# An output norm by two full-width ones-matmuls, one table set in the RWKV mixer, and work of ACT, DVE, POOL and PE moved at three stage borders

## The chip, the cores and the metric

The kernel runs on one core of one Trainium2 chip. The metric is the device time of one execution in microseconds (us). TensorE is written PE, VectorE DVE, ScalarE ACT, GpSimd POOL, SyncE SP.

## The reference

The input is 512 tokens by 1024 features, in float32. A first block (a gated convolution beside a state-space branch) is followed by two layers, each of them FFN, mixer, FFN; the mixer of layer 0 is a convolution beside RWKV-7, that of layer 1 is attention. Cut to what matters:

```python
def rms_norm(x, g):
    return x * lax.rsqrt(jnp.mean(x * x, axis=-1, keepdims=True) + 1e-6) * g

def hybrid_layer(x, pre_g, w_in, ..., w_out, post_g):      # the first block
    proj = rms_norm(x, pre_g) @ w_in
    ca, cb, z_c, u_s, z_s, g_c, g_s = split(proj)
    conv_out = (silu(layer_norm(conv(ca * sigmoid(cb)))) * silu(z_c)) @ w_conv_out
    y = gelu(s5_mimo(u_s, ...))
    y = y * sigmoid(y @ w_glu + b_glu)
    ssm_out = (y * silu(z_s)) @ w_ssm_out
    out = (sigmoid(g_c) * conv_out + sigmoid(g_s) * ssm_out) @ w_out
    return x + rms_norm(out, post_g)                       # the output norm

for layer in range(2):
    x = x + 0.5 * swiglu(rms_norm(x, g[0]), w_gate[layer, 0], w_up[layer, 0], w_down[layer, 0])
    x = x + mixer[layer](rms_norm(x, g[1]))                # RWKV and conv, then attention
    x = x + 0.5 * swiglu(rms_norm(x, g[2]), w_gate[layer, 1], w_up[layer, 1], w_down[layer, 1])

# in the RWKV mixer
kk = kk * lax.rsqrt(jnp.maximum(jnp.sum(kk * kk, axis=-1), 1e-24))
y = (y - mu) * lax.rsqrt(var + 64e-5) * ln_w + ln_b        # group norm over a head
```

## The kernel before

Activations lie transposed: eight tiles of 128 features by 512 tokens (`xT`). A product of float32 precision is made of two parts of each operand, a high one (the operand rounded to the PE's format) and a low one (what is left), in three rounds of matmuls: high weight by high activation, high weight by low activation, low weight by high activation. So each norm tile is made twice, `hH` by ACT (L388, L1420) and `hL` by DVE (L392, L1590). Each "unit" of weights, up to eight blocks of 128x128 that make one output tile, is loaded by SP into `w_raw`, split by ACT into `w_hi` (`split_hi`, L313) and by POOL into `w_lo` (`split_lo`, L321). The gate and up weights of an FFN are split by ACT (`gu_hi`, L607) and DVE (`gu_lo`, L616).

The work of every engine is one list of instructions, written out by hand, which runs in order; semaphores order the engines among each other. A `wait_ge` stops the engine, and all that stands behind it in its list. The changed lists stand at these places:

- **Start of block 1.** PE transposes `x_in`, ACT makes the eight `hH` (L1420), DVE the eight `hL`. PE then runs unit 0 (L1885, L1889, L1892: the three rounds), `raw_x(0)` (L1921, sixteen transposes that ACT copies to `xT`, L1432), unit 1, `params`, `raw_x(1)`, unit 2, the transposes of `srow` (L1941), unit 3, those of `Bblk` (L1949), unit 4. Between them ACT computes two sines (L1467, L1469), and DVE from these a chain of eleven small operations on `srow`, each of which waits for the one before it (L1642 to L1662); L1941 reads its last result. From unit 4 hang the state-space matrices and the convolution of the first block.
- **Output norm of block 1.** ACT squares each output tile (L1564), DVE adds the squares up (L1838). PE sums over the features by matmuls with a matrix of ones, one column per 128 tokens (L2051, L2054), ACT takes the root of a 128x4 tile (L1571), DVE its reciprocal (L1843) and four diagonal matrices (L1846), and PE spreads them over all rows (L2059) into `bank[7]`. DVE multiplies by it (`o_scale`, L1850), DVE (L1855) or POOL (L1382) adds the residual, and ACT and DVE make `hH` and `hL` of the first FFN.
- **First FFN (e = 0).** The first four gate/up units are "plain" (`plain_front` L1074 to L1086, `plain_back` L1098 to L1103), 512 tokens at once; later ones work on combined half-width tiles. For each unit DVE scales the gate by the norm's root R (`scale`, L877), ACT applies SiLU (L728), DVE multiplies by the up part (`gated`, L889), ACT makes the high part (`high`, L732), POOL the low part (L688). `norm_pe` (L423) sums the squares, ACT makes R by `Ln` and `Exp` (L738, L740). DVE also makes the sums that the combined units need (`state_sums`, L638 to L642; `turned_sum` L653; L588 to L592 on weights).
- **RWKV mixer.** For each of four head pairs, the preparation takes exponentials for the decays (L2267) and the root of the norm of `kk` (L2290, L2292). Then come triangular inverses over a chunk's tokens in levels, for two halves w = 0 and 1: PE L2757, L2777, with masks by POOL (L2238), while ACT, DVE make the group norm (L2323, L2328) of finished halves. POOL splits the units of the output product, `U_EO` and on, in between. The mixer ends with `group_affine` (L2338), `mix_hi` (L2313), the output product (L339 to L346), the residual (L2656) and the norm tiles of the next FFN; between these ACT and POOL split the last units, `U_EO + 4` and on. The gate/up units of the FFN behind (L1074 and on) follow.

## Time and profile before

| what | value |
|---|---|
| median of 3 runs | 2393.78 us (2391.64 to 2393.97) |
| the profiled execution | 2392.06 us |
| its span, from the first to the last instruction | 2390.2 us |
| mean granted TensorE clock | 0.998 |
| busy share of the span: PE, DVE, ACT, POOL | 98%, 71%, 47%, 37% |
| table loads of ACT | 48, each 1283 ns |

The span is the profiled execution less 1.9 us of start and end. A busy share counts the time in which an engine executes. In a row of the timeline the first number is when an instruction (or a run of equal ones, with "x" and their count) began, the second how long it lasted, and the brackets at the end say how long the engine had sat idle before it and what ended this.

### The profile page before, as it was taken

How to read it: one execution, taken by the hardware profiler on the slowest of the kernel's cores; microseconds unless marked ns; L12 is line 12 of the kernel's file. 1: busy time of each engine (PE TensorE's matmuls, PEld its weight loads, DVE VectorE, ACT ScalarE, POOL GpSimd, SP SyncE). 2: the span in 40 equal slices, each digit the busy share in tenths (PEclk: the TensorE clock that was granted, in tenths of full speed). 3: DMA queues.
4: the chain of work that ended last, by engine and by line, in shares of the span. 5: the costliest groups of instructions: out<-in, count | busy, mean ns of one | idle time of the engine just before them, and what ended most of it. 6: DMA issues, size and time to landing. Idle time of an engine off the chain costs nothing.

```text
span 2390.2 us, 42066 instructions
## 1 busy us (share of the span) xinstructions
PE 2335.4 (98%) x16891; PEld 1983.2 (83%) x16891; DVE 1698.9 (71%) x2282; ACT 1130.3 (47%) x1738; POOL 879.6 (37%) x533
## 2 busy tenths in 40 slices
PE   8999999999999999989999999999999999999999
PEld 6667767789899887877898998998998557898997
DVE  6999984297486479865884876865855776884771
ACT  5433353466265335334662654653644344562552
POOL 3799945322413446522114123132134212114123
PEclk9999999999999999999999999999999999999999
DMA  5222214223433332002334333342334221334333
GB/s 161 71 75 76 80 58 125 83 84 90 119 107 96 110 97 78 27 4 59 106 96 126 89 94 110 107 120 84 107 98 106 58 54 53 89 96 126 89 90 96
DMA packets 420789, 214.46 MB, mean 90 GB/s; under 512 B 17317, under 2 KB 419035, under 8 KB 420603
## 3 DMA queue, kind: packets, MB, share of 16 engines
q1 hardware_dynamic: 416523, 209.05, 30.9%
q10 hardware_dynamic: 4080, 2.83, 0.5%
q8 instruction: 129, 2.11, 0.4%
q14 instruction: 57, 0.47, 0.1%
HBM read 209.22 MB, written 2.10 MB: 88 GB/s over the span
## 4 chain that ended last, share of the span: by engine, by line
PE 76%; DVE 12%; POOL 7%; issue 2%; ACT 2%; DMA 0%; POOLq 0%; ACTq 0%; DVEq 0%
PE bank L1008 11%; PE bank L1014 10%; PE bank L1026 10%; PE bank L339 9%; PE bank L346 9%; PE bank L343 9%; POOL w_lo L321 3%; PE bank L1892 2%; PE bank L1889 2%; PE bank L1885 2%; DVE bank L1719 1%; PE bank L3436 1%; PE bank L2777 1%; POOL tmp L1352 1%; POOL tmp L1350 1%
## 5 line engine op out<-in xcount | busy, mean ns | idle before, releaser
L321 POOL TENSOR_TENSOR w_lo<-w_raw,w_hi 128x1024 fp32r<-128x1024 f32 (+5 forms) x276 | 534.5, 1942 | 568.4 <-ACT w_hi L313 566.1
L616 DVE TENSOR_TENSOR gu_w_lo<-gu_w,gu_w_hi 128x1024 fp32r<-128x1024 f32 (+1 forms) x254 | 364.1, 1436 | 92.4 <-ACT gu_w_hi L607 91.8
L688 POOL TENSOR_TENSOR ffn_aL<-tmp,ffn_aH 128x512 fp32r<-128x512 f32 x88 | 132.9, 1511 | 733.9 <-ACT ffn_aH L732 733.9
L313 ACT ACTIVATE w_hi<-w_raw 128x1024 fp32r<-128x1024 f32 (+5 forms) x276 | 235.8, 856 | 289.2 <-PE bank L346 272.5
L607 ACT ACTIVATE gu_w_hi<-gu_w 128x1024 fp32r<-128x1024 f32 (+1 forms) x254 | 299.5, 1183 | 30.2 <-DVE gu_w L590 19.4
L1008 PE MATMUL bank<-hH,gu_w_hi 128*128 128x256 f32 x1248 | 300.0, 279 | 0.0
L1014 PE MATMUL bank<-hL,gu_w_hi 128*128 128x256 f32 x1248 | 299.0, 279 | 0.0
L1008 PEld LDWEIGHTS bank<-hH,gu_w_hi 128*128 128x128 f32 x1248 | 231.5, 188 | 1.1 <-ACT tmp L724 0.5
L978 DVE TENSOR_TENSOR bank<-bank,R 128x512 f32<-128x512 f32 x64 | 44.7, 699 | 263.6 <-PE bank L346 263.6
L1014 PEld LDWEIGHTS bank<-hL,gu_w_hi 128*128 128x128 f32 x1248 | 231.0, 188 | 0.1
L1008 PE MATMUL bank<-st_hi,gu_w_hi 128*128 128x256 f32 x936 | 225.8, 280 | 1.1 <-ACT tmp L724 1.1
L1014 PE MATMUL bank<-st_lo,gu_w_hi 128*128 128x256 f32 x936 | 225.6, 280 | 0.0
L724 ACT ACTIVATE tmp<-bank 128x256 f32<-128x256 f32 x312 | 118.1, 378 | 181.0 <-PE bank L1026 180.9
L1026 PE MATMUL bank<-hH,gu_w_lo 128*128 128x256 f32 x1248 | 195.0, 278 | 0.0
L339 PE MATMUL bank<-ffn_aH,w_hi 128*128 128x512 f32 x704 | 181.1, 390 | 0.0
L346 PE MATMUL bank<-ffn_aH,w_lo 128*128 128x512 f32 x704 | 180.9, 390 | 0.0
L343 PE MATMUL bank<-ffn_aL,w_hi 128*128 128x512 f32 x704 | 180.4, 389 | 0.0
L1008 PEld LDWEIGHTS bank<-st_hi,gu_w_hi 128*128 128x128 f32 x936 | 173.5, 188 | 1.7 <-ACT tmp L724 1.7
L1014 PEld LDWEIGHTS bank<-st_lo,gu_w_hi 128*128 128x128 f32 x936 | 173.5, 188 | 0.0
L1026 PEld LDWEIGHTS bank<-hH,gu_w_lo 128*128 128x128 f32 x1248 | 167.1, 188 | 0.0
L1719 DVE SCALAR_TENSOR_TENSOR bank<-cu,par,bank 128x512 f32<-128x512 f32 x232 | 160.2, 741 | 0.0
L346 PEld LDWEIGHTS bank<-ffn_aH,w_lo 128*128 128x128 f32 x704 | 131.5, 188 | 28.6 <-POOL w_lo L321 1.6
(563 smaller groups left out, 4673.2 us busy)
## 6 DMA issues: line engine op xcount, KB each, us to landing
gu_w<-in_ffn_w_gate SPq DMA_DIRECT2D x88, 512.0 KB, 3.7
gu_w<-in_ffn_w_up SPq DMA_DIRECT2D x88, 512.0 KB, 4.8
w_raw<-in_w_in SPq DMA_DIRECT2D x48, 512.0 KB, 3.8
w_raw<-in_ffn_w_down SPq DMA_DIRECT2D x64, 384.0 KB, 3.6
w_raw<-in_ffn_w_down SPq DMA_DIRECT2D x64, 320.0 KB, 3.3
w_raw<-in_even_w_in SPq DMA_DIRECT2D x26, 512.0 KB, 3.9
w_raw<-in_w_conv_out SPq DMA_DIRECT2D x8, 512.0 KB, 4.0
w_raw<-in_w_out SPq DMA_DIRECT2D x8, 512.0 KB, 3.8
```

Of the source, the lines that this page charges most:

```text
L313: nc.scalar.activation(w_hi[u % 3][:, 0:K, :], w_raw[u % 4][:, 0:K, :], ACT.Identity).then_inc(w_hi_ready, 1)
L321: nc.gpsimd.tensor_tensor(w_lo[u % 3][:, 0:K, :], w_raw[u % 4][:, 0:K, :], w_hi[u % 3][:, 0:K, :].bitcast(F32), ALU.subtract).then_inc(w_l ...
L339: nc.tensor.matmul(out, H[:, k, :], sH[:, k0 + k, :], start=start and k == 0, stop=False)
L343: nc.tensor.matmul(out, H[:, k, :], sL[:, k0 + k, :], start=False, stop=False)
L346: ins = nc.tensor.matmul(out, L[:, k, :], sH[:, k0 + k, :], start=False, stop=stop and k == K - 1)
L607: nc.scalar.activation(gu_wh[v % 2][:, b0:b1, :, :], gu_w[v % 3][:, b0:b1, :, :], ACT.Identity).then_inc(gu_hi_ready, 1)
L616: nc.vector.tensor_tensor(gu_wl[v % 3][:, b0:b1, :, :], gu_w[v % 3][:, b0:b1, :, :], gu_wh[v % 2][:, b0:b1, :, :].bitcast(F32), ALU.subtra ...
L688: nc.gpsimd.tensor_tensor(aL[:, in_half(n), :], up_t[:, :], aH[:, in_half(n), :].bitcast(F32), ALU.subtract).then_inc(a_lo, 1)
L1008: nc.tensor.matmul(out, H[:, block, k, :], state_hi_lo(operand, k)[0], start=name in OPENS and k == 0, stop=False, skip_group_check=True)
L1014: nc.tensor.matmul(out, H[:, block, k, :], state_hi_lo(operand, k)[1], start=False, stop=False, skip_group_check=True)
L1026: ins = nc.tensor.matmul(out, L[:, block, k, :], state_hi_lo(operand, k)[0], start=False, stop=k == 3, skip_group_check=True)
L1719: ins = V.scalar_tensor_tensor(x_ if k == PAD else acc, x_, w_, acc, M, A)
```

## The change

1. **Start.** PE interleaves units 0 and 1 (`first_two`): for each of the eight `hH` a matmul of unit 0 and one of unit 1, the same over `hL`, then the low weights of unit 0, then those of unit 1. `raw_x(0)` comes behind both. ACT splits unit 1 ahead of the eight `hH`.
2. **Output norm.** Two ones-matmuls of 128x512 sum the squares over the features and leave the sum in every row; ACT makes the inverse root by `Ln` and `Exp` on 128x512. The column matmuls, the root of 128x4, the reciprocal, and the four diagonal matrices with their matmuls go. DVE's first `gu_lo` of unit 1 moves behind four low tiles, ACT's second `gu_hi` of unit 1 behind the first `hH`.
3. **First FFN.** `plain_front` waits for banks and weights one by one, where it uses them; `norm_pe` moves into the second unit's back part, between its gate and its up half; SiLU, `high` and copies on ACT, and `gated`, `scale`, `turned_sum` on DVE change places in the third to fifth unit.
4. **RWKV.** One table set, which holds the logarithm and the exponential, is loaded ahead of the decays; 12 of the 48 table loads go (8 at `kk`, 4 at the group norm).
5. **POOL's** splits of units `U_EO` and `U_EO + 1` move from before the masks of half 0 to between the halves.
6. **RWKV's tail.** ACT runs both `group_affine` of the last pair at once, and both `mix_hi` with one split between them; the splits of units `U_EO + 8` and `+ 9` come one norm tile earlier.

```diff
@@ ACT, first FFN
                 gu_hi(act, 1, 0)
-                gu_hi(act, 1, 1)
                 for j0 in (0, 4):
                     for j in range(j0, j0 + 4):
                         high_tile(act, gain(0, j), j, x_tile_new(j))
+                        if j == 0:
+                            gu_hi(act, 1, 1)
...
                         if e == 0 and v == 2:
+                            silu(n - 1)
                             state_high_act(act, e, 3)
+                            high(n - 1)
+                            continue
...
+                        if e == 0 and v == 3:
+                            turned_high_act(act, e)
+                            gu_hi(act, n + 1, 2)
+                            continue
...
+                    if e == 0 and c == 0 and v == 4:
+                        silu(n - 2)
+                        high(n - 2)
+                        gu_hi(act, n + 1, 0)
+                        copy(n, COPIES[1])
+                        silu(n - 1)
+                        copy(n, COPIES[2])
+                        high(n - 1)
+                        gu_hi(act, n + 1, 1)
+                        copy(n, COPIES[3])
+                        gu_hi(act, n + 1, 2)
+                        copy(n, COPIES[4])
+                        continue
@@ DVE, first FFN
                             state_sums_dve(v, e, 3)
+                            gated(n - 1)
                             gu_lo(v, n + 1, 0)
                             gu_lo(v, n + 1, 1)
-                            gated(n - 1)
...
+                        if e == 0 and v_ == 3:
+                            turned_sum_dve(v, e)
+                            scale(n - 1)
+                            gu_lo(v, n + 1, 1)
+                            turned_low_dve(v, e)
+                            gated(n - 1)
+                            continue
@@ PE, plain units
-            for n in ns:
-                ring_free(pe, n)
-                for which in range(2):
-                    free_banks(pe, n, which)
-                    pe.wait_ge(gu_hi_ready, part_no(n, which))
             for k in range(4):
                 pe.wait_ge(h_hi, q + k + 1)
                 for n in ns:
+                    if k == 0:
+                        ring_free(pe, n)
                     for which, block in ((0, 0), (1, 5)):
+                        if k == 0:
+                            free_banks(pe, n, which)
+                            pe.wait_ge(gu_hi_ready, part_no(n, which))
...
                             plain_back(pe, n)
-                            norm_pe(pe)
                         else:
-                            plain_back(pe, n)
+                            plain_back(pe, n, between=norm_pe)
@@ ACT, first block
             split_hi(act, 0)
+            split_hi(act, 1)
             act.wait_ge(setup_rd, PRE_RD)
             for j in range(DT):
                 act.wait_ge(setup_ps, XS_PS + j + 1)
                 s.activation(hH[:, j, :], bank[j][:, :], ACT.Identity, scale=pc("pre", j)).then_inc(h1_hi, 1)
-            split_hi(act, 1)
...
                 if j == 6:
-                    s.activation(rowst[:, 12:13], small[:, 0:1], ACT.Sqrt).then_inc(act_step, 1)
-                    act_sent(act_step)
+                    s.preload_act_table_set("natural_log_exp_and_others")
             act.wait_ge(ln_ps, O_PS)
-            s.activation(rowst[:, 0:4], bank[0][:, 0:4], ACT.Sqrt, scale=1.0 / D, bias=EPS6).then_inc(o_sq, 1)
+            s.activation(tmp[4][:, :], bank[7][:, :], ACT.Ln, scale=1.0 / D, bias=EPS6).then_inc(act_step, 1)
+            act.wait_ge(act_step, act_sent(act_step))
+            s.activation(bank[7][:, :], tmp[4][:, :], ACT.Exp, scale=-0.5).then_inc(o_sq, 1)
@@ DVE, output norm
-            v.wait_ge(o_sq, DT + 1)
-            V.reciprocal(rowst[:, 4:8], rowst[:, 0:4]).then_inc(dve_step, 1)
-            v.wait_ge(dve_step, dve_sent(dve_step))
-            for m_ in range(TT):
-                V.tensor_scalar(tmp[4][:, m_ * P:(m_ + 1) * P], ident[:, :], rowst[:, 4 + m_:5 + m_], None, M).then_inc(ln_gated, 1)
...
-            gu_lo(v, 1, 0)
-            v.wait_ge(ln_ps, R_PS)
+            v.wait_ge(o_sq, DT + 1)
...
                 if j0 == 0:
+                    gu_lo(v, 1, 0)
                     gu_lo(v, 1, 1)
@@ PE, first block
-            pe.wait_ge(h1_lo, 1)
-            w_in_unit(0, ready=(h1_lo, 0))
+            def first_two():
+                pe.wait_ge(h1_lo, 1)
+                pe.wait_ge(w_hi_ready, 1)
+                for k in range(DT):
+                    pe.wait_ge(h1_hi, k + 1)
+                    mm(w_in_bank(0)[:, :], w_hi[0][:, k, :], hH[:, k, :], start=k == 0, stop=False)
+                    if k == 0:
+                        pe.wait_ge(h1_lo, 2)
+                        pe.wait_ge(w_hi_ready, 2)
+                    mm(w_in_bank(1)[:, :], w_hi[1][:, k, :], hH[:, k, :], start=k == 0, stop=False)
+                for k in range(DT):
+                    pe.wait_ge(h1_lo, k + 1)
+                    for u in range(2):
+                        mm(w_in_bank(u)[:, :], w_hi[u][:, k, :], hL[:, k, :], start=False, stop=False)
+                for u in range(2):
+                    pe.wait_ge(w_lo_ready, u + 1)
+                    for k in range(DT):
+                        ins = mm(w_in_bank(u)[:, :], w_lo[u][:, k, :], hH[:, k, :], start=False, stop=k == DT - 1)
+                    ins.then_inc(unit_done, 1)
+
+            first_two()
             raw_x(0)
-            w_in_unit(1)
...
-            pe.wait_ge(o_sq, 5)
             pe.wait_ge(o_sum, DT - 2)
-            for m_ in range(TT):
-                mm(bank[0][:, m_:m_ + 1], tmp[3][:, m_ * P:(m_ + 1) * P], ones[:, 0:1], start=True, stop=False)
-                if m_ == 0:
-                    pe.wait_ge(o_sq, DT)
-                ins = mm(bank[0][:, m_:m_ + 1], tmp[7 % 3][:, m_ * P:(m_ + 1) * P], ones[:, 0:1], start=False, stop=True)
-            ins.then_inc(ln_ps, 1)
-            pe.wait_ge(o_sq, DT + 1)
-            for m_ in range(TT):
-                pe.wait_ge(ln_gated, DIAG + m_ + 1)
-                mm(bank[7][:, m_ * P:(m_ + 1) * P], ones[:, :], tmp[4][:, m_ * P:(m_ + 1) * P], start=True, stop=True).then_inc(ln_ps, 1)
+            mm(bank[7][:, :], ones[:, :], tmp[3][:, :], start=True, stop=False)
+            pe.wait_ge(o_sq, DT)
+            mm(bank[7][:, :], ones[:, :], tmp[7 % 3][:, :], start=False, stop=True).then_inc(ln_ps, 1)
@@ POOL, RWKV
-            for u in range(U_EO, U_EO + 2):
-                split_lo(pool, u)
             for w in range(2):
+                if w:
+                    for u in range(U_EO, U_EO + 2):
+                        split_lo(pool, u)
@@ ACT, RWKV
+                s.preload_act_table_set("natural_log_exp_and_others")
                 act.wait_ge(rw["csum"], J + 1)
...
             group_affine(1, 0)
+            group_affine(1, 1)
             split_hi(act, U_EO + 4)
-            group_affine(1, 1)
             act.wait_ge(rw["done"], 3)
             mix_hi(6, rT[:, 2, :])
-            split_hi(act, U_EO + 5)
             act.wait_ge(rw["done"], 4)
             mix_hi(7, rT[:, 3, :])
+            split_hi(act, U_EO + 5)
...
-                if U_EO + n_ + 2 < U_F[1]:
+                if n_ not in (6, 7) and U_EO + n_ + 2 < U_F[1]:
                     split_hi(act, U_EO + n_ + 2)
+                if n_ in (5, 6):
+                    split_hi(act, U_EO + n_ + 3)
```

The lists of PE at the start, where a row is an instruction with its line, its output and inputs and its count, read before:

```order
L1885 MATMUL bank<-hH,w_hi_55 128x512 x8
L1889 MATMUL bank<-hL,w_hi_55 128x512 x8
L1892 MATMUL bank<-hH,w_lo_57 128x512 x8
L1921 MATMUL bank<-ident,x_in 128x128 x16
L1885 MATMUL bank<-hH,w_hi_56 128x512 x8
L1889 MATMUL bank<-hL,w_hi_56 128x512 x8
L1892 MATMUL bank<-hH,w_lo_58 128x512 x8
L1927 MATMUL bank<-ident,prow 128x128 x2
```

and in the changed kernel, whose lines have other numbers (L1912 is L1885 of before, L1948 is L1921, L1954 is L1927; "..." leaves out the pairs that follow in the same way, over `hH` and then over `hL`):

```order
L1962 MATMUL bank<-hH,w_hi_55 128x512
L1966 MATMUL bank<-hH,w_hi_56 128x512
...
L1974 MATMUL bank<-hH,w_lo_57 128x512 x8
L1974 MATMUL bank<-hH,w_lo_58 128x512 x8
L1948 MATMUL bank<-ident,x_in 128x128 x16
L1954 MATMUL bank<-ident,prow 128x128 x2
L1948 MATMUL bank<-ident,x_in 128x128 x16
L1912 MATMUL bank<-hH,w_hi_59 128x512 x8
```

The first `raw_x` (sixteen `x_in` transposes) moved from behind unit 0 to behind unit 1; `params` (`prow`) stands directly ahead of the second `raw_x`, as before.

DVE's list at the output norm before, from the reciprocal on:

```order
L1843 RECIPROCAL rowst<-rowst 128x4
L1846 TENSOR_SCALAR tmp_70<-ident,rowst 128x128 x4
L616 TENSOR_TENSOR gu_w_lo_82<-gu_w_79,gu_w_hi_85 128x1024
L1850 TENSOR_TENSOR oT<-oT,bank 128x512
L1855 TENSOR_TENSOR xT<-xT,oT 128x512
L1850 TENSOR_TENSOR oT<-oT,bank 128x512 x2
L1855 TENSOR_TENSOR xT<-xT,oT 128x512
L1850 TENSOR_TENSOR oT<-oT,bank 128x512
L392 SCALAR_TENSOR_TENSOR hL<-xT,par,hH 128x512 x4
L616 TENSOR_TENSOR gu_w_lo_82<-gu_w_79,gu_w_hi_85 128x1024
```

and in the changed kernel, from the first multiplication of the output by the root on:

```order
L1877 TENSOR_TENSOR oT<-oT,bank 128x512
L1882 TENSOR_TENSOR xT<-xT,oT 128x512
L1877 TENSOR_TENSOR oT<-oT,bank 128x512 x2
L1882 TENSOR_TENSOR xT<-xT,oT 128x512
L1877 TENSOR_TENSOR oT<-oT,bank 128x512
L392 SCALAR_TENSOR_TENSOR hL<-xT,par,hH 128x512 x4
L616 TENSOR_TENSOR gu_w_lo_82<-gu_w_79,gu_w_hi_85 128x1024 x2
```

The reciprocal and four diagonal tiles are gone, and the split of `gu_w_lo_82` moved from ahead of the first multiplication to behind the four low tiles `hL`.

ACT's list at the end of the RWKV mixer before, from the first of the last two mixed tiles on (`w_hi` 128x256 and 128x1024 are splits of units, `hH` and the squares in `tmp` the norm tiles):

```order
L2313 ACTIVATE mixH<-rT 128x512
L313 ACTIVATE w_hi_56<-w_raw_54 128x256
L2313 ACTIVATE mixH<-rT 128x512
L313 ACTIVATE w_hi_59<-w_raw_51 128x256
L388 ACTIVATE hH<-xT,par 128x512
L378 ACTIVATE tmp_69<-xT 128x512
L313 ACTIVATE w_hi_55<-w_raw_52 128x256
L388 ACTIVATE hH<-xT,par 128x512
L378 ACTIVATE tmp_67<-xT 128x512
L313 ACTIVATE w_hi_56<-w_raw_53 128x1024
L388 ACTIVATE hH<-xT,par 128x512
L378 ACTIVATE tmp_68<-xT 128x512
```

and in the changed kernel, from the same tile on:

```order
L2352 ACTIVATE mixH<-rT 128x512 x2
L313 ACTIVATE w_hi_56<-w_raw_54 128x256
L313 ACTIVATE w_hi_59<-w_raw_51 128x256
L388 ACTIVATE hH<-xT,par 128x512
L378 ACTIVATE tmp_69<-xT 128x512
L313 ACTIVATE w_hi_55<-w_raw_52 128x256
L313 ACTIVATE w_hi_56<-w_raw_53 128x1024
L388 ACTIVATE hH<-xT,par 128x512
L378 ACTIVATE tmp_67<-xT 128x512
L313 ACTIVATE w_hi_59<-w_raw_54 128x1024
L388 ACTIVATE hH<-xT,par 128x512
```

The two mixed tiles now follow each other, and the splits of 128x1024 into `w_hi_56` and `w_hi_59` moved ahead of the norm tiles 1 and 2 that they stood behind.

## Rows read from the trace of the kernel before

**Rows 1.** The page, busy time of each engine over the span.

```profile
PE 2335.4 (98%) x16891; PEld 1983.2 (83%) x16891; DVE 1698.9 (71%) x2282; ACT 1130.3 (47%) x1738; POOL 879.6 (37%) x533
```

**Rows 2.** Busy time in two stretches: PE, PEld, DVE, ACT, POOL, granted clock, DMA, GB/s.

```profile
85.00:307.00 222.00, 216.78 (x918) 155.64 (x916) 221.92 (x325) 80.44 (x113) 214.57 (x143) 1.00 0.26 74
...
476.00:478.00 2.00, 2.00 (x6) 1.56 (x5) 2.00 (x3) 0.52 (x1) 1.45 (x1) 0.51 0.04 8
```

**Rows 3.** The timeline of PE at the start.

```profile
15.89 3.67 PE L1885 MATMUL bank<-hH,w_hi 128*128 128x512 f32 x8 [0.95 <-DVE hL L1590]
...
19.40 2.00 PE L1889 MATMUL bank<-hL,w_hi 128*128 128x512 f32 x8
...
23.07 1.91 PE L1921 MATMUL bank<-ident,x_in 128*128 128x128 f32 x16
...
37.81 0.42 PE L1941 MATMUL bank<-ident,srow 16*128 16x16 f32 x4
...
45.56 0.71 PE L1885 MATMUL bank<-hH,w_hi 128*128 128x512 f32 x2
```

**Rows 4.** The timeline of ACT, DVE and POOL at the start.

```profile
27.78 0.29 ACT L1469 ACTIVATE srow<-srow 16x128 f32<-16x128 f32 x1
...
31.77 0.27 DVE L1642 TENSOR_TENSOR srow<-srow 16x128 f32<-16x128 f32 x1
...
34.52 2.38 DVE L1660 TENSOR_TENSOR srow<-srow 16x128 f32<-16x128 f32 x1
...
36.93 0.28 DVE L1662 TENSOR_TENSOR srow<-srow 16x128 f32<-16x128 f32 x1
...
34.22 2.53 POOL L321 TENSOR_TENSOR w_lo<-w_raw,w_hi 128x1024 fp32r<-128x1024 f32 x1 [2.74 <-ACT w_hi L313]
```

**Rows 5.** The timeline at the output norm, and L738, L740 of the next norm.

```profile
466.20 0.38 PE L2054 MATMUL bank<-ones,tmp 128*128 128x1 f32 x2 [0.57 <-ACT tmp L1564]
...
469.05 2.05 PE L2059 MATMUL bank<-tmp,ones 128*128 128x128 f32 x8 [1.05 <-DVE tmp L1846]
...
469.40 1.22 DVE L616 TENSOR_TENSOR gu_w_lo<-gu_w,gu_w_hi 128x1024 fp32r<-128x1024 f32 x1
...
471.13 0.69 DVE L1850 TENSOR_TENSOR oT<-oT,bank 128x512 f32<-128x512 f32 x1 [0.51 <-PE bank L2059]
...
496.56 0.67 ACT L738 ACTIVATE tmp<-bank,small 128x512 f32<-128x512 f32 x1
...
497.26 0.63 ACT L740 ACTIVATE R<-tmp 128x512 f32<-128x512 f32 x1
```

**Rows 6.** The timeline of PE and DVE in the first FFN.

```profile
493.30 1.13 PE L423 MATMUL bank<-tmp,ones 128*128 128x512 f32 x2 [0.74 <-DVE tmp L383]
...
512.14 2.08 PE L1074 MATMUL bank<-hH,gu_w_hi 128*128 128x512 f32 x8 [1.01 <-issue]
...
532.24 0.73 PE L1008 MATMUL bank<-hH,gu_w_hi 128*128 128x256 f32 x4
...
511.85 2.25 DVE L588 TENSOR_TENSOR gu_w<-gu_w 128x1024 f32<-128x1024 f32 x1
```

**Rows 7.** The timeline in the RWKV mixer, DVE and PE.

```profile
968.98 2.88 DVE L2495 TENSOR_TENSOR prep<-prep,prep 128x512 f32<-128x512 f32 x1
...
977.96 1.16 PE L2757 MATMUL bank<-a_w,b_w 64*64 64x64 f32 x64 [0.34 <-DVE vT L2437]
```

**Rows 8.** The timeline at the RWKV mixer's end, ACT, DVE and PE.

```profile
1105.05 1.28 ACT L2328 ACT_TABLE_LOAD   x1
...
1106.34 1.15 ACT L2328 ACTIVATE tmp<-tmp 128x512 f32<-128x512 f32 x2
...
1123.69 1.45 DVE L392 SCALAR_TENSOR_TENSOR hL<-xT,par,hH 128x512 fp32r<-128x512 f32 x1 [0.86 <-ACT hH L388]
...
1122.16 2.11 PE L339 MATMUL bank<-mixH,w_hi 128*128 128x512 f32 x8 [1.11 <-ACT w_hi L313]
...
1155.89 2.19 PE L1074 MATMUL bank<-hH,gu_w_hi 128*128 128x512 f32 x8
```

13 lines of the change are left out of this document (9 added, 4 removed).

## Prediction

> **What bounds the kernel now.** I read the page's busy shares first: PE is busy for 2335.4 us of a span of 2390.2, 98% [rows 1]. All that a reordering can give is the remaining 55 us, and only where a wait of PE is removed and not made again behind it. Then I read the busy time by stretches, to see where another engine sets the pace. From 85 to 307 us DVE is busy for 221.92 of 222.00 us and POOL for 214.57 [rows 2]: there DVE decides, and PE (216.78) follows. So the start, which comes before that stretch, is worth exactly what it moves DVE's full stretch, whose input comes from unit 4 of PE at 45.56 [rows 3]. The list of PE's waits then gave the other places: the output norm, three plain units, the RWKV mixer and its end [rows 5 to 8]. No edit touches the long stretches in which PE is full.
>
> One thing in the trace bears on nearly all edits. DVE's chain at the start has steps of 0.27 to 0.28 us at 31.77 and 36.93, but the step at 34.52 lasted 2.38 [rows 4]. POOL had begun a `w_lo` at 34.22 that lasted 2.53, to 36.75, and the DVE step ended at 36.90, with it. The same shows in other stages: a 128x1024 operation of DVE that takes 1.22 at 469.40 [rows 5] took 2.25 at 511.85 [rows 6], and a 128x512 one of the preparation took 2.88 at 968.98 [rows 7]. So a DVE step on tiles in SBUF waits for a POOL operation that is under way; what is moved in time may be gained on PE and lost there.
>
> **The change part by part.** The sum is made against the profiled execution, 2392.06 us, which is 1.72 under the median of 2393.78; what the sum gives I add to the median.
>
> *Start.* The first eight matmuls over `hH` took from 15.89 to 19.40, 3.51, and the two dense rounds behind them from 19.40 to 23.07, 1.83 each [rows 3]: 1.68 of waiting for ACT. In the changed list sixteen matmuls share the eight `hH`. They need 3.66 dense; ACT makes the last `hH` at about 19.4, and two matmuls follow it, so they end near 19.9, and 0.35 of waiting stays. PE gains 1.68 - 0.35 = **1.3** by the end of unit 1. Against this, `raw_x(0)`, which began at 23.07 [rows 3], comes one unit later, about 27.2: ACT, which copies it and then makes two sines, of which the second ended at 28.07 [rows 4], has them at 23.07 to 27.2 = 4.1 less what its queue had in reserve, some 3.3 later: 31.35. That alone costs nothing, since DVE began on them only at 31.77 [rows 4]. But ACT's next weight split stands behind the sines, and with it POOL's `w_lo`: one now lies at about 32.5 to 34.9 and one at 35.45 to 37.85, and the chain of eleven DVE steps, which met one, meets both. Eleven steps of 0.31 (a step with its gap: 31.77 to 34.52 are nine) with two blocked ones end near 38.9; they ended at 37.21. L1941, which began at 37.81, begins at about 39.1 where PE is ready at 36.45. PE had no slack there, so the 1.3 is lost, and unit 4 begins at 46.2 to 46.4 where it began at 45.56 [rows 3]: **+0.8**. Ends: -1.3 if the second POOL operation misses the chain; if the next chain on DVE is hit as well, two blocked steps of 2.1 each (2.38 - 0.28) less the gain, +2.9. I take the replay.
>
> *Output norm.* Before: the column matmuls began their last part at 466.20, the spreading matmuls at 469.05, and DVE's first multiplication started at 471.13 [rows 5]. After: the last of two ones-matmuls begins at 466.20; a pair of these took 1.13 [rows 6], so I take 1.0; `Ln` and `Exp` cost 0.67 and 0.63 on the same shape [rows 5]; with the hand-overs `o_scale` starts at 468.65, 2.5 earlier. Behind it stands DVE: its `gu_lo` of 1.22 lay in the hole at 469.40 [rows 5] and now stands behind four low tiles with nothing to hide it. What reaches the second half of the norm is 2.5 - 1.2 = **1.3**. The granted clock adds a limit: it was 0.51 in 476 to 478 [rows 2], the lower level of 1.2 GHz after PE had stood still before these matmuls, and PE stands still at the new norm too; what PE does earlier there it does at that level.
>
> *First FFN.* If PE follows DVE's lead, its waits of 0.74 at 493.30 and 1.01 at 512.14 [rows 6] go as well: -1.3 - 0.74 - 1.01 = -3.1, the lower end. But DVE is the one that is full here, and its lead is 1.3. POOL's `st_lo` get ahead of DVE's steps as at 511.85, where one such meeting cost 2.25 - 1.22 = 1.0 [rows 6]; two more would leave -1.3 + 2.0 = +0.7, the upper end. I follow the chain to the matmul at 532.24 [rows 6], where the combined units' copies on ACT stand behind SiLU, `high` and weight splits, and take **-1.2** for norm and FFN together, near DVE's own lead. From 545 on PE is full and carries this to the mixer. The cover for the added Ln and Exp on ACT is nil, they are in the chain and in the sum; ACT's moved `gu_hi` lies in its waits for `hH`.
>
> *RWKV.* Eight loads fewer in the preparation (1.28 each [rows 8]) are hidden: ACT waits for DVE in each pair. In the last pair they let DVE end earlier; it ran late, blocked by four `w_lo`, as the row of 2.88 shows, and PE waited 0.34 for it at 977.96 [rows 7] and shortly at three places behind. Both loads of the last pair are worth at most 2 x 1.28 = 2.6, and nothing if POOL's lock hides them again. Loads of the group norm between two levels free some tenths more. The two moved `w_lo` of POOL now lie beside DVE's level steps of half 0's end, where one blocked step costs up to 2.1, of which I let 0.4 through, since DVE waits for PE there anyway. Together **-1.0** (ends: -2.6 and +0.5).
>
> *The mixer's end.* ACT's load at 1105.05 (1.28) lay between the root of the group norm and all that follows, and PE waited 1.11 at 1122.16 for the split of `U_EO + 8` [rows 8]. Both go: -2.4, the lower end. But POOL's `w_lo` follow ACT's splits. They come one tile earlier, among the low tiles and sums of DVE's norm: the low tile at 1123.69 lasted 1.45 beside such a `w_lo` [rows 8], twice the 0.69 that a step of as many elements takes at 471.13 [rows 5]. In my replay the two moved `w_lo` block one step each of 1.2 to 1.5, and the first unit of the next FFN, PE at 1155.89 [rows 8], which hangs on this DVE chain through ACT's weight split, comes 1.3 *later*. Between -2.4 and +1.3 I take **0**.
>
> Sum: +0.8 - 1.2 - 1.0 + 0 = **-1.4**; 2393.8 - 1.4 = **2392.4 us** (and 2390.7 if a profiled execution again lies 1.7 below).
>
> **The page on table loads.** The switch row shows a load of 1.28 at 1105.05 and the next ACTIVATE at 1106.34, 0.01 behind it [rows 8]. The Trainium skill ("ScalarE: Activation LUTs", section "What ACT_TABLE_LOAD costs") puts a switch at about 2.7 us with the engine's drain. By it the one exposed load would be worth 1.4 more, and the sum would be -2.8; by the row it is -1.4. The row measures this kernel, so I use it.
>
> **Rivals.** A measurement here can tell about 0.2%, 4.8 us, from no change.
>
> - *The gaps close on PE (chance 0.15).* No new DVE step is blocked: -1.3 - 3.1 - 1.0 - 2.4 = -7.8, 2386.0. For it: each of these waits stands in a row. Against it: DVE is the bound at two of the four places. Partly so, two places of four (another 0.17): some -5 to -6, 2388.
> - *VectorE and GpSimd collide at every border (0.08 over the bound, and 0.14 within it).* Start +2.9, FFN +0.7, mixer 0, mixer's end +1.3: +4.9, 2398.7. It decides from two further blocked steps of 2.1 at the start, since DVE is full from 85 to 307 [rows 2] and hands on every delay. The Trainium skill states it as a rule ("SBUF — State Buffer", section "Who interferes with whom"): an operation of VectorE with two inputs in SBUF and one of GpSimd that reads SBUF exclude each other for a whole instruction, and the one that started first goes on. Row 34.52 agrees with it.
> - *Nothing of it arrives (0.05).* All edits lie beside PE's work or are cancelled in the next wait: 2393.8. Against it: the waits at 1122.16 and 512.14 have their cause in the moved items.
> - *A switch of tables costs ScalarE longer than its row (0.02).* With a drain as long as the load, 12 loads free 31 us of ACT, but only the exposed one counts: -1.4 more, 2391.0.
>
> **Numbers.** The forecast itself (partly cancelled gains) has 0.39. Faster by over 0.2% (under 2389.0): 0.32. Slower by over 0.2% (over 2398.6): 0.08. Within: 0.39 + 0.14 + 0.05 + 0.02 = 0.60. The range goes down to the first rival, 2386.0, and up by the collisions short of their full sum, +3.0 on the median, 2396.8; about one in ten lies below and one in ten above.
>
> **What would show it.** In the changed trace: the `srow` transposes of PE near 39.1 with two DVE steps over 1.5 us in the chain, unit 4 near 46.3; the first `o_scale` at 468.3 to 469.5 and the following `gu_lo` after the fourth low tile; PE's L423 without wait, the third plain unit about 1 us earlier; no wait of PE for `w_hi` at the mixer's end, but low tiles or sums of 1.2 to 2.4 us there. It is wrong if the chain at the start meets one POOL operation only (then about -2.1 more), if PE, not DVE, turns out to set the first FFN (-1.9 more), or if the first gate/up unit behind the mixer comes earlier by more than 2 us beyond what the places before it gave.

## The result, and the profile after

The changed kernel takes 2400.51 us (median of 10 runs, 2397.36 to 2402.18), the kernel before 2393.33 (10 runs, 2391.64 to 2394.95): +7.2 us, a ratio of 1.0028 with an interval of 1.0020 to 1.0036. It is slower, by more than the 4.8 us that I took as the bound, and outside my range of 2386.0 to 2396.8. Its profiled execution took 2401.15, which is 9.1 over the profiled execution of before (2392.06): the first lies 0.6 over its median and the second 1.3 under its own, so the shifts read from the two traces are together 1.9 more than the difference of the times.

The page of the changed kernel, its span and the busy time of each engine, against [rows 1]:

```profile
span 2399.3 us, 42006 instructions
...
PE 2336.3 (97%) x16871; PEld 1985.2 (83%) x16871; DVE 1701.0 (71%) x2277; ACT 1115.3 (46%) x1726; POOL 878.0 (37%) x533
```

PE does the same work (2336.3 us against 2335.4) in a span that is 9.1 longer, so the time went into waits and a little into a lower clock. To see where, I took the start of the same matmul in both traces. The numbers are the start after less the start before:

| stretch | matmul of before, at | shift of the changed kernel | change over the stretch |
|---|---|---|---|
| start | unit 4, 45.3 | +5.6 | +5.6 |
| first block | 460 | +5.5 | -0.1 |
| norm, three plain units | 523.2 | +2.3 | -3.2 |
| first combined units | 532.2, then 545 | +5.1, then +6.7 | +2.8, then +1.6 |
| long full stretch | 960 | +6.7 | 0.0 |
| RWKV mixer | 1112 | +7.3 | +0.5 |
| end of the mixer | 1122.2 | +4.7 | -2.6 |
| next FFN | 1155.9, then 1200 | +8.2, then +9.1 | +3.5, then +1.0 |
| to the last unit | 1600 | +9.1 | 0.0 |

A shift that falls is a gain on PE. At the start PE ends unit 2 1.4 us earlier, at the norm and at the end of the mixer the table shows gains of 3.2 and 2.6, and each of the three is followed by a larger loss. The stretches by engine show DVE still full from 85 to 307, and the granted clock in two places where it was 1.00 before:

```profile
85.00:307.00 222.00, 216.63 (x916) 155.15 (x915) 222.00 (x326) 77.96 (x109) 211.59 (x141) 1.00 0.26 75
...
42.00:49.00 7.00, 7.00 (x20) 5.54 (x21) 4.44 (x10) 0.00 (x0) 1.28 (x1) 0.62 0.26 74
...
538.00:542.00 4.00, 4.00 (x24) 4.00 (x24) 4.00 (x6) 0.95 (x4) 0.00 (x0) 0.60 0.39 107
```

**The start.** The timeline of PE, then DVE's chain on `srow` (L1675 to L1695, before L1642 to L1662), then POOL, against [rows 3, 4]:

```profile
34.45 1.98 PE L1919 MATMUL bank<-hH,w_lo 128*128 128x512 f32 x8
41.33 0.60 PE L1986 MATMUL bank<-ident,srow 16*128 16x16 f32 x4 [4.91 <-DVE srow L1695]
41.86 3.78 PE L1912 MATMUL bank<-hH,w_hi 128*128 128x512 f32 x8
...
51.18 2.10 PE L1912 MATMUL bank<-hH,w_hi 128*128 128x512 f32 x8
```

```profile
31.64 0.28 DVE L1675 TENSOR_TENSOR srow<-srow 16x128 f32<-16x128 f32 x1 [1.24 <-ACT srow L1501]
...
32.83 2.38 DVE L1683 TENSOR_TENSOR srow<-srow 16x128 f32<-16x128 f32 x1
...
35.56 2.43 DVE L1687 TENSOR_TENSOR srow<-srow 16x128 f32<-16x128 f32 x1
...
38.65 2.31 DVE L1693 TENSOR_TENSOR srow<-srow 16x128 f32<-16x128 f32 x1
41.00 0.28 DVE L1695 TENSOR_TENSOR srow<-srow 16x128 f32<-16x128 f32 x1
```

```profile
32.63 2.44 POOL L321 TENSOR_TENSOR w_lo<-w_raw,w_hi 128x1024 fp32r<-128x1024 f32 x1 [8.33 <-ACT w_hi L313]
35.49 2.36 POOL L321 TENSOR_TENSOR w_lo<-w_raw,w_hi 128x1024 fp32r<-128x1024 f32 x1 [0.42 <-ACT w_hi L313]
38.34 2.48 POOL L321 TENSOR_TENSOR w_lo<-w_raw,w_hi 128x1024 fp32r<-128x1024 f32 x1 [0.49 <-ACT w_hi L313]
```

PE ends unit 2 at 36.4, 1.4 earlier than before. DVE's chain begins at 31.64, as it did at 31.77. But a split of POOL is under way at 32.83, at 35.56 and at 38.65, and each time one step of 0.28 lasts until that split is over: 2.38, 2.43 and 2.31. PE stands still for 4.91 us, and then its granted clock is at the lower level of 1.2 GHz: the first dense round of unit 3 takes 3.78, where the same round of before took 2.11. The transposes start 3.5 us later than before (41.33 against 37.81), and unit 4, the next unit but one, starts 5.6 later: 51.18 where it started at 45.56. So 2.1 of the 5.6 come behind the wait, from the lower clock.

**The norm.** PE, ACT and DVE, against [rows 5]:

```profile
471.74 1.11 PE L2096 MATMUL bank<-tmp,ones 128*128 128x512 f32 x2
...
472.89 0.69 ACT L1602 ACTIVATE tmp<-bank,small 128x512 f32<-128x512 f32 x1 [0.64 <-PE bank L2096]
473.61 0.60 ACT L1604 ACTIVATE bank<-tmp 128x512 f32<-128x512 f32 x1
...
474.30 0.69 DVE L1877 TENSOR_TENSOR oT<-oT,bank 128x512 f32<-128x512 f32 x1 [6.77 <-ACT bank L1604]
...
482.42 2.35 DVE L616 TENSOR_TENSOR gu_w_lo<-gu_w,gu_w_hi 128x1024 fp32r<-128x1024 f32 x2
```

From PE's first matmul behind the last square to the first `o_scale` it takes 474.30 - 471.74 = 2.56 us; before it was 471.13 - 466.20 = 4.93. That is 2.4 less, and 2.5 was forecast. Both `gu_lo` now stand one behind the other at 482.42 (2.35 for the two), in DVE's way. The second half's first `o_scale` starts at 484.69, 4.3 later than before, where PE had come to the norm 5.5 later: 1.2 is left, and 1.3 was forecast.

**The first FFN.** PE, ACT, DVE and POOL at the first combined units, against [rows 6]:

```profile
537.38 0.73 PE L1039 MATMUL bank<-hH,gu_w_hi 128*128 128x256 f32 x4 [3.17 <-ACT tmp L724]
...
527.46 0.62 ACT L728 ACTIVATE tmp<-tmp 128x512 f32<-128x512 f32 x1
...
535.05 0.63 ACT L732 ACTIVATE ffn_aH<-tmp 128x512 fp32r<-128x512 f32 x1 [3.25 <-DVE tmp L910]
535.59 1.47 ACT L607 ACTIVATE gu_w_hi<-gu_w 128x1536 fp32r<-128x1536 f32 x1
536.96 0.36 ACT L724 ACTIVATE tmp<-bank 128x256 f32<-128x256 f32 x1
...
530.64 2.33 DVE L588 TENSOR_TENSOR gu_w<-gu_w 128x1024 f32<-128x1024 f32 x1
...
534.34 0.68 DVE L910 TENSOR_TENSOR tmp<-tmp,bank 128x512 f32<-128x512 f32 x1
...
529.54 2.34 POOL L688 TENSOR_TENSOR ffn_aL<-tmp,ffn_aH 128x512 fp32r<-128x512 f32 x1 [10.44 <-ACT ffn_aH L732]
```

PE waits 3.17 us for a copy (L724, 536.96) that stands on ACT behind a split of 1.47 and behind `high` of the fourth unit, which waits for `gated` on DVE at 534.34. DVE is late there because `gated` of the third unit had to wait for a SiLU that ACT now runs at 527.46, behind the turned tiles, and because L588 met a `low` of POOL (2.33 at 530.64, where it lasts 1.21 alone). Behind the wait the clock is 0.60 for 4 us, which costs 1.6 more.

**The end of the mixer.** PE, DVE and POOL, against [rows 8]:

```profile
1126.81 1.98 PE L339 MATMUL bank<-mixH,w_hi 128*128 128x512 f32 x8
...
1157.95 0.50 PE L1129 MATMUL bank<-hH,gu_w_hi 128*128 128x512 f32 x1 [2.16 <-ACT hH L388]
...
1126.87 2.31 DVE L392 SCALAR_TENSOR_TENSOR hL<-xT,par,hH 128x512 fp32r<-128x512 f32 x1 [1.04 <-ACT hH L388]
1129.10 2.88 DVE L383 TENSOR_TENSOR tmp<-tmp,tmp 128x512 f32<-128x512 f32 x1
...
1126.22 2.41 POOL L321 TENSOR_TENSOR w_lo<-w_raw,w_hi 128x1024 fp32r<-128x1024 f32 x1 [0.21 <-ACT w_hi L313]
1129.02 2.41 POOL L321 TENSOR_TENSOR w_lo<-w_raw,w_hi 128x1024 fp32r<-128x1024 f32 x1 [0.39 <-ACT w_hi L313]
```

PE's wait for `w_hi` at 1122.16 of before is gone: the matmul starts 2.6 us earlier in relation to what stands ahead of it. Half of this, 1.3, is there by 1116, ahead of that wait. But the `w_lo` at 1126.22 and 1129.02 hold DVE's low tile for 2.31 and its sum for 2.88, where 0.75 and 0.68 are what they last alone. The norm tiles of the next FFN come later, PE waits 2.16 for one at 1157.95 and the third plain unit begins at 1164.06.

### The profile page after: what moved, and what is told of

Its sections match the earlier page's. It is cut to its first block, busy times and chain, and to the rows that moved or that the text cites. A ratio compares the mean times of both kernels' runs of the same rounds, so it can differ in the third digit from the quotient of the medians.

```text
span 2399.3 us, 42006 instructions
## 1 busy us (share of the span) xinstructions
PE 2336.3 (97%) x16871; PEld 1985.2 (83%) x16871; DVE 1701.0 (71%) x2277; ACT 1115.3 (46%) x1726; POOL 878.0 (37%) x533
## 3 DMA queue, kind: packets, MB, share of 16 engines
q8 instruction: 129, 2.11, 0.4%
## 4 chain that ended last, share of the span: by engine, by line
PE 83%; POOL 8%; DVE 5%; issue 2%; ACT 1%; DMA 0%; POOLq 0%; ACTq 0%; DVEq 0%
PE bank L339 11%; PE bank L346 11%; PE bank L343 11%; PE bank L1039 11%; PE bank L1045 11%; PE bank L1057 10%; POOL w_lo L321 3%; PE bank L1912 2%; PE bank L1919 2%; PE bank L1916 1%; DVE bank L1752 1%; PE bank L3477 1%; PE bank L1105 1%; POOL tmp L1384 1%; POOL tmp L1382 1%
## 5 line engine op out<-in xcount | busy, mean ns | idle before, releaser
L724 ACT ACTIVATE tmp<-bank 128x256 f32<-128x256 f32 x312 | 118.1, 379 | 183.8 <-PE bank L1057 183.7
```

## The experiments

All were timed in five rounds beside the kernel before, on one chip for each group of four. The differences are medians of 11 runs less the median of the 33 runs of before of the same group (2393.13, 2392.51 and 2393.37). Their intervals are about 2.2 us to each side. So beside each time stands the shift of PE's matmuls in the one profiled execution. Within a short stretch it tells small effects apart that the times don't; from 960 to 1112 us it can't, since executions differ by over 1 us there, as shown below.

### e1: the start alone

```diff
+            split_hi(act, 1)          # ahead of the eight hH
-            w_in_unit(0, ready=(h1_lo, 0))
+            first_two()
             raw_x(0)
-            w_in_unit(1)
```

> The kernel before with the start alone changed: PE interleaves units 0 and 1, ACT splits unit 1 ahead of the eight hH. Theory (three POOL splits block DVE's chain on srow, PE stands still at the srow transposes and then runs at the lower clock): unit 4 begins 5 to 6 us later than in the kernel before (51.2 against 45.56), and as DVE is full behind it, the whole kernel takes 5 to 6 us more, 2398 to 2400. Rival (the start's delay is swallowed before 460 us, and the loss of the changed kernel comes from the later stages): under 1.5 us more.

Measured: 2398.75, +5.6 us, ratio 1.0023 (1.0014 to 1.0032). PE of this kernel behind the chain:

```profile
41.40 0.60 PE L1959 MATMUL bank<-ident,srow 16*128 16x16 f32 x4 [4.90 <-DVE srow L1662]
```

The round of unit 3 behind it again takes 3.78. The shift is +5.7 at unit 4 and +5.5 at 960. The theory holds and the rival falls: only 0.2 of it is swallowed, since DVE is full behind it. The start alone is over the bound of 4.8 us.

### e2: everything but the start

```diff
-            first_two()
+            w_in_unit(0, ready=(h1_lo, 0))
             raw_x(0)
+            w_in_unit(1)
```

> The changed kernel with the start as it was. Theory (the start holds about 5.6 of the loss): 1 to 3 us over the kernel before, 2394.5 to 2396.5. Rival (the loss is in the norm, the first FFN and the end of the mixer): 5 us or more over it, 2398 or more.

Measured: 2393.35, +0.2 us, ratio 1.0000 (0.9991 to 1.0009). Below the 1 to 3 that I expected, and far from the rival. Its profiled execution took 2395.05, 1.7 over its median, and its matmuls end 3.0 later than those of before. In its trace the later stages win and lose as in the changed kernel: -3.4 to 523 us, +2.8 and +1.6 in the combined units, -2.6 and +3.5 at the end of the mixer.

### e3 and e8: the end of the mixer

e3 makes the whole of this part in the kernel before; e8 leaves the splits of units `U_EO + 8` and `+ 9` where they were:

```diff
             group_affine(1, 0)
+            group_affine(1, 1)
             split_hi(act, U_EO + 4)
-            group_affine(1, 1)
...
-                if U_EO + n_ + 2 < U_F[1]:            # e3 alone
+                if n_ not in (6, 7) and U_EO + n_ + 2 < U_F[1]:
                     split_hi(act, U_EO + n_ + 2)
+                if n_ in (5, 6):
+                    split_hi(act, U_EO + n_ + 3)
```

> The kernel before with only ACT's list at the end of the RWKV mixer changed (both affine steps and both mixed tiles together, the splits of two units one norm tile earlier). Theory (the earlier w_lo on POOL block a low tile and a sum on DVE, 2.3 and 2.9 us long where 0.7 is usual): PE's first matmul behind the eight-block units comes 1 to 2 us earlier, but the first gate/up unit of the next FFN about 3 us later; +2.5 to +3.5, 2396 to 2397. Rival (those long steps come from the table loads and the later start, not from the moved splits): no more than +0.5.

> As e3, but without the splits of two units moved one norm tile earlier: only both affine steps together and both mixed tiles together. Theory (the moved splits alone block DVE's low tile and sum): no step over 1.5 us on DVE between 1116 and 1130, the wait of PE for the last mixed tile gone, the wait for w_hi of about 1.1 stays or grows; total 0 to -1.5. Rival (the mixed tiles' new order causes the loss): +1 or more.

Measured: e3 2394.23, +1.1 us, ratio 1.0005 (0.9996 to 1.0014), and e8 2391.55, -1.0 us, 0.9993 (0.9984 to 1.0002). Neither is clear of no change by its time. DVE in e3:

```profile
1121.37 2.30 DVE L392 SCALAR_TENSOR_TENSOR hL<-xT,par,hH 128x512 fp32r<-128x512 f32 x1 [1.04 <-ACT hH L388]
...
1125.93 2.31 DVE L392 SCALAR_TENSOR_TENSOR hL<-xT,par,hH 128x512 fp32r<-128x512 f32 x1 [0.94 <-ACT hH L388]
```

DVE and PE in e8:

```profile
1120.49 0.75 DVE L392 SCALAR_TENSOR_TENSOR hL<-xT,par,hH 128x512 fp32r<-128x512 f32 x1 [0.87 <-ACT hH L388]
1121.16 0.68 DVE L383 TENSOR_TENSOR tmp<-tmp,tmp 128x512 f32<-128x512 f32 x1
...
1121.90 2.12 PE L339 MATMUL bank<-mixH,w_hi 128*128 128x512 f32 x8 [1.11 <-ACT w_hi L313]
```

In e3 two low tiles last 2.3 us; in e8 the same low tile and the sum behind it last 0.75 and 0.68, and PE's wait of 1.11 for `w_hi` stays. From 1112 to 1200 us PE loses 1.3 in e3 and gains 1.0 in e8. So the splits, moved to spare PE a wait of 1.1, cost 2.4, and the mixed tiles together with both affine steps bring 1.0. The theory on the blocked steps holds. Its +2.5 to +3.5 for e3's time was too much: +1.1 is the median, +1.3 the shift over the stretch. e8 lies in its expected range.

The 1.0 is gained by 1116, where PE of before waits for the last mixed tile. This is the same wait that the load at 1105.05 [rows 8] lengthens: e12, with the load gone and the old order, gains 1.3 there, and the four kernels with both (the changed one, e2, e9, e10) gain 1.3 too, not 2.3. So beside the new table set the order of the mixed tiles is worth nothing, and of the changed kernel's end of the mixer the splits cost more than in e3: from 1116 to 1200 us it loses 3.2, e3 2.3.

### e4 and e7: the norm and the first FFN

e4 makes the norm and all edits of the first FFN in the kernel before. e7 leaves the lists of ACT and DVE at the fourth and fifth unit as before:

```diff
-                        if e == 0 and v == 3:         # taken out again in e7
-                            turned_high_act(act, e)
-                            gu_hi(act, n + 1, 2)
-                            continue
...
-                        if e == 0 and v_ == 3:
-                            turned_sum_dve(v, e)
-                            scale(n - 1)
...
-                    if e == 0 and c == 0 and v == 4:
-                        silu(n - 2)
-                        high(n - 2)
...
```

> The kernel before with the output norm and the first FFN changed, nothing else. Theory (the norm gains 1.3 on DVE and up to 3.3 on PE, and the first combined unit gives it back in one wait of PE for a copy that stands behind high and a weight split on ACT): -3.3 at the first combined unit, +0.5 to +1.2 at 545 us; total +0.5 to +1.2, 2394 to 2394.6. Rival (the wait in the changed kernel was a consequence of the late start): total -2 to -3.3, 2390 to 2391.5.

> As e4 (output norm and first FFN), but with the lists of ACT and DVE at the fourth and fifth unit as before: SiLU and high of the third unit ahead of the turned highs. Theory (the wait of 3.2 us at the first combined units' fourth product comes from SiLU of the third unit having moved behind the turned tiles, so that gated 3 on DVE and high 3 on ACT came 5 us late): that wait is at most 1 us, PE is 2 to 3 us ahead of the kernel before at 545 us and does not fall to the lower clock there; total -2 to -3. Rival (DVE is full there and gives the same back in another wait): within 0.5 of e4's time.

Measured: e4 2395.43, +2.3 us, ratio 1.0009 (1.0000 to 1.0018); e7 2392.76, +0.2 us, 1.0002 (0.9992 to 1.0011). PE in e7, all its waits between 512 and 545 us:

```profile
524.47 0.74 PE L1012 MATMUL bank<-st_hi,gu_w_hi 128*128 128x256 f32 x4 [1.29 <-ACT tmp L724]
...
528.02 0.74 PE L1012 MATMUL bank<-hH,gu_w_hi 128*128 128x256 f32 x4 [0.46 <-ACT tmp L724]
...
530.25 0.72 PE L1012 MATMUL bank<-st_hi,gu_w_hi 128*128 128x256 f32 x4 [0.58 <-ACT tmp L724]
```

One wait of 3.2 became three of 1.29, 0.46 and 0.58, and the clock stays up. Against its own shift at 460, e4 has -3.5 at 523, -0.7 at 532 and +1.0 at 545; e7 has -3.2, -0.5 and -0.5. e4's shifts came as expected, its time is 1.1 over the expected range, and its rival falls. Of e7 my theory was half right. The changed lists of the fourth and fifth unit make the wait that lets the clock fall, 1.7 us; e7 takes all of them out at once, and that the moved SiLU is the one among them rests on the rows of the changed kernel. They don't explain why the gain of 3 is gone by 532: that happens with the old lists as well. e7 is not the 2 to 3 us ahead at 545 that I expected, nor is its time 2 to 3 us shorter. The rival's other waits are there, though its number (within 0.5 of e4's time) is not, and "full" is too strong: DVE is busy for 10.18 of the 12 us from 520 to 532 in e7, and the copies for which PE waits stand on ACT behind steps that wait for DVE. What it would take to keep the gain was not tried.

### e5, e6 and e11: what makes the start slow

All three are e1 with one thing more. In e5 the sines go ahead of the copies of x:

```diff
             after_unit(0)
-            x_copy(0)
             act.wait_ge(arg_ready, 2)
             s.activation(srow[0:PAIRS, 9, :], srow[0:PAIRS, 7, :], ACT.Sin, ...)
             s.activation(srow[0:PAIRS, 10, :], srow[0:PAIRS, 8, :], ACT.Sin, ...)
+            x_copy(0)
```

In e6 DVE's chain on `srow` also goes ahead of its copies of the parameters, behind the first `cu`:

```diff
+            cu_mul(0)
+            v.wait_ge(row_root, SIN_DONE)
+            V.tensor_tensor(r(12), r(4), r(10), M)    # the chain, eleven steps
...
             v.wait_ge(setup_ps, PAR01_PS)
             V.tensor_scalar(par[:, cw_:cw_ + TAPS * DT], bank[2][...], 0.5, None, M)
-            cu_mul(0)
-            v.wait_ge(row_root, SIN_DONE)
```

In e11 all stands as in e1, and POOL's operation for units 3, 4 and 5 is short; it leaves out the low weights of these units but for 16 columns:

```diff
+            if u in (3, 4, 5):
+                nc.gpsimd.tensor_tensor(w_lo[u % 3][:, 0, 0:16], w_raw[u % 4][:, 0, 0:16], ...)
+                return
```

> The start alone changed as in e1, and the two sines on ACT moved ahead of the copies of x. Theory (the number of POOL splits that fall into DVE's chain on srow decides): the chain begins at about 30.4 instead of 31.6, DVE's params and cu being ahead of it, and meets one or two splits instead of three; unit 4 begins 1 to 3 us later than in the kernel before, total +1 to +3. Rival (the chain was late because the transposes of x and its copies are late, however POOL works): it would be no better than the 1.2 us earlier start gives, unit 4 +4.4, total +4.4.

> As e5, and DVE's chain on srow moved ahead of its params copies, behind the first cu. Theory: the chain runs from about 28 to 31.5, between POOL's third and fourth split, so that no step is blocked; PE keeps its gain of 1.3 at the srow transposes, unit 4 begins at 44.2 to 44.8; total -0.8 to -1.4. Rival (PE waits for something else there, for instance the bank that params and cu free): unit 4 no earlier than 45.56, total 0 or more.

> As e1 (the start alone), but POOL computes only 16 columns of the low weights of units 3, 4 and 5, so that its operations there are short; the low part of these three units is left out of the product. Nothing else is moved. Theory (a step of DVE waits for the end of the POOL operation under way): no step of DVE's chain on srow over 0.5 us, the srow transposes begin when PE is ready, at about 36.5, unit 4 at 44.2 to 44.8, no stretch at the lower clock at the start; total -1 to -1.5 instead of e1's +5.6. Rival (the chain is late because of ACT's later sines): the long steps go, but the chain still ends after 37.8, unit 4 at 45.5 or later, total 0 or more.

Measured: e5 2393.18, +0.7 us, ratio 1.0002 (0.9993 to 1.0011). e6 2392.00, -0.5 us, 0.9999 (0.9990 to 1.0008). e11 2392.01, -1.4 us, 0.9993 (0.9984 to 1.0002). DVE and PE of e5:

```profile
31.41 2.35 DVE L1646 TENSOR_SCALAR srow<-srow 16x128 f32<-16x128 f32 x1
...
34.41 2.36 DVE L1652 TENSOR_TENSOR srow<-srow 16x128 f32<-16x128 f32 x1
...
38.40 0.41 PE L1959 MATMUL bank<-ident,srow 16*128 16x16 f32 x4 [1.51 <-DVE srow L1662]
```

Of e6, whose chain begins at 27.76, the chain's last step and unit 4; its transposes begin at 36.10, without a wait:

```profile
30.82 2.39 DVE L1657 TENSOR_TENSOR srow<-srow 16x128 f32<-16x128 f32 x1
...
43.66 2.07 PE L1884 MATMUL bank<-hH,w_hi 128*128 128x512 f32 x8
```

Of e11, the chain's first step, the transposes and unit 4:

```profile
32.06 0.28 DVE L1646 TENSOR_TENSOR srow<-srow 16x128 f32<-16x128 f32 x1 [1.23 <-ACT srow L1473]
...
36.78 0.42 PE L1963 MATMUL bank<-ident,srow 16*128 16x16 f32 x4
...
43.93 2.09 PE L1889 MATMUL bank<-hH,w_hi 128*128 128x512 f32 x8
```

The number of blocked steps in the chain sets unit 4: three, +5.7 (e1); two, +0.1 (e5); one, and that one in the slack, -1.9 (e6); none, -1.6 (e11). In e11 ACT's sines are as late as in e1 and the chain starts at 32.06 (31.64 in the changed kernel); it still ends at 35.42, before PE is ready, and no wait is left. So the late sines alone cost nothing; what costs is the splits that the chain meets, and the sines decide only which ones those are. From e1 to e5 the transposes come 3.0 earlier: 0.9 by the chain's earlier start (30.78 against 31.71) and 2.1 by one blocked step less. With two blocked steps PE's wait was 1.51 and its clock stayed at 1.00, and from the transposes to unit 4 PE took 7.3 us; in e1 it took 9.9 (before 7.8, with a wait of 0.4). So the third step costs more than its own 2.1: with it come 2.6 us of the lower clock.

e5's chain met two splits, the upper count of my theory, and yet unit 4 and the time came earlier than its ranges (+0.1 where I had 1 to 3, +0.7 where I had +1 to +3). e6's chain was to meet none and met one, in its last step; unit 4 at 43.66 is earlier than I expected, and its time (-0.5) falls short of -0.8 to -1.4. e11 came as its theory says (unit 4 0.3 earlier), and its rival falls.

e6 keeps its -1.9 up to 960 us, where it is -2.2, and has -1.0 at 1112. All eight kernels with the old RWKV lists (e1, e3 to e8, e11) lose 0.7 to 1.7 over that stretch against the profiled execution of before; its time, 2392.06, was below its median by 1.3. That execution was short in the mixer, so the shifts there are against a low mark.

### e12: the RWKV mixer alone

```diff
+                s.preload_act_table_set("natural_log_exp_and_others")
                 act.wait_ge(rw["csum"], J + 1)
...
-            for u in range(U_EO, U_EO + 2):
-                split_lo(pool, u)
             for w in range(2):
+                if w:
+                    for u in range(U_EO, U_EO + 2):
+                        split_lo(pool, u)
```

> The kernel before with only the RWKV mixer's part changed: one table set, and POOL's two splits moved between the halves. Theory (DVE ends the last pair's preparation earlier, and PE's waits behind it shrink): PE gains 0.8 to 1.4 between 960 and 1112 us against the kernels with the old lists, of which seven lost 0.7 to 1.7 there against the one trace of the kernel before; total -0.5 to -1.5. Rival (nothing of the removed loads was on the path): 0.

Measured: 2390.58, -2.8 us, ratio 0.9987 (0.9978 to 0.9996). This is more than I expected, and beside e1 the one part that is clear by its own time. Its profiled execution took 2392.61, 2.0 over its median: at 1028 to 1035 the granted clock was 0.54, where it was 1.00 in the kernel before,

```profile
1028.00:1035.00 7.00, 5.81 (x205) 5.46 (x204) 3.47 (x8) 1.09 (x2) 1.98 (x2) 0.54 0.02 6
```

so its shift of +1.3 from 960 to 1112, where a gain of 0.8 to 1.4 against the old lists was expected, says little of the lists. Shorter stretches say more. From 960 to 980 us PE gains 1.0 in each of the five kernels with the new lists (the changed one, e2, e9, e10, e12) and nothing (under 0.1) in the eight with the old ones. POOL and DVE of the kernel before:

```profile
965.59 10.22 POOL L321 TENSOR_TENSOR w_lo<-w_raw,w_hi 128x1024 fp32r<-128x1024 f32 x4
...
971.89 2.21 DVE L2497 TENSOR_TENSOR b_w<-prep,prep 128x512 f32<-128x512 f32 x1
...
974.86 1.50 DVE L2501 TENSOR_TENSOR yc<-tmp,tmp 128x512 f32<-128x512 f32 x1
```

and of e12:

```profile
965.98 5.73 POOL L321 TENSOR_TENSOR w_lo<-w_raw,w_hi 128x1024 fp32r<-128x1024 f32 x2
...
972.29 0.69 DVE L2499 TENSOR_TENSOR b_w<-prep,prep 128x512 f32<-128x512 f32 x1
...
973.74 0.69 DVE L2503 TENSOR_TENSOR yc<-tmp,tmp 128x512 f32<-128x512 f32 x1
```

Where four splits stood, two are left, and the two DVE steps that waited for the others last 0.69. PE's wait of 0.34 at 977.96 [rows 7] goes with them. DVE's steps ahead of these keep their distance to PE (e12's are 0.4 later, as PE is), though ACT has two table loads fewer there. So the gain of 1.0 comes from POOL's two moved splits, and the removed loads of the preparation bring nothing.

From 1112 to 1122 e12 gains 1.3: the load of 1.28 that stood at 1105.05 [rows 8] is on the path, at its full price. On ACT the step from the last `Ln` to the first `Exp` shrinks by 1.4 (from 1104.35 to 1106.34 before, from 1106.13 to 1106.71 in e12), so nothing like a second 1.28 hides behind the load. Together these are -2.3, near the -2.8 of the time. What the new lists do between 980 and 1112 the traces don't show: the five with them lose 0.8 to 2.7 there, the eight without 0.7 to 1.7.

### e9 and e10: the parts that pay, together

e9 is the start of e6, the norm and FFN of e7, e12, and e8. e10 is the same with the first FFN's lists as before:

```diff
-                            silu(n - 1)               # e10 against e9, ACT, third unit
                             state_high_act(act, e, 3)
-                            high(n - 1)
-                            continue
...
-                            plain_back(pe, n, between=norm_pe)
+                            plain_back(pe, n)
...
```

> The parts that cost nothing together: the start as in e6, the output norm with the first FFN as in e7, the RWKV tables and POOL's two splits as in the changed kernel, and the end of the mixer as in e8. Theory (the places add, each with what its own trace showed by the position of PE's matmuls: -2.0, -0.5, -1.1, -1.0): -4 to -5 us, 2388 to 2389. Rival (what one place gains the next one swallows, as the mixer did with a third of e6's gain): -1 to -2.

> As e9, but with the lists of the first FFN all as before; the new output norm stays. Theory (the norm's gain reaches PE through DVE's lead of 1.3 whatever the FFN's order, and the FFN's order gives its gain back in the same stage): within 1 us of e9. Rival (the reordered FFN lists carry the gain): 1.5 us or more over e9.

Measured: e9 2389.87, -3.5 us, ratio 0.9986 (0.9977 to 0.9995). e10 2388.60, -4.8 us, ratio 0.9979 (0.9970 to 0.9988), the fastest version of the study and 11.9 under the changed kernel (2400.51, timed in another group). e9 falls between theory and rival; e8's 1.0 doesn't come beside the load's 1.3, as said above. e10's time is 1.3 under e9's, a little more than the 1 us expected; their traces end within 0.2 of each other. The rival falls. In e10 the norm's gain shows by itself: the shift goes from -1.3 at 460 to -2.5 at 503 and is still -2.6 at 960. So the new norm is worth 1.2, the lead of DVE. In e9 the reordered FFN goes to -4.5 at 523 and is back at -1.4 from 532 on: it gives back not only its own gain but 0.9 of the norm's.

## Why the prediction was wrong

The forecast was 2392.4 and the time 2400.5, 8.1 more. Stage by stage, in shifts of the changed kernel's trace (together 9.1): start +5.5 for a forecast of +0.8, norm and first FFN +1.2 for -1.2, RWKV +0.6 for -1.0, the end of the mixer +1.8 for 0. Every term came out worse, and the start by most; the RWKV figure is read against the low mark told under e6.

**The start, the step that failed.** I forecast +0.8, with -1.3 to +2.9 as its ends; it is +5.6 (e1). What I worked out for PE (1.3 earlier) and for the sines held: the second ended at 31.60, forecast 31.35. The chain on DVE was replayed with the two POOL splits that I had placed, at 32.5 and 35.45; they came at 32.63 and 35.49. With these two the chain was to end near 38.9. The third split began at 38.34, in the middle of what was left of the chain. My replay had not placed it, because before it stood at 39.5, after the chain. The replay's own numbers could have told: its two splits are 2.95 apart, and a third at the same distance begins at 38.4, ahead of 38.9. A chain that is held up by POOL's operations lasts longer and so meets more of them; I stopped one short. And PE's wait then grew to 4.91, with the lower clock behind it, of which the sum had nothing: 2.1 us against the kernel before. The upper end was built from two blocked steps of the next chain, so it couldn't hold this.

**The rule on the shared port.** The second rival (collisions of VectorE and GpSimd) is what happened, and I gave it 0.08 over the bound; even its full sum, 2398.7, is 1.8 short. The runs agree with what the Trainium skill says ("SBUF — State Buffer", section "Who interferes with whom"), that the operation that started first holds the other for its whole length: with 128x1024 splits a step of 0.28 that became ready just behind their start lasts 2.3 to 2.4, with 128x16 ones (e11) 0.28. It decided at the start, as that rival said, though through a third meeting in the first chain and not through the second chain.

**The norm.** Right in mechanism and size: -2.4 to the first `o_scale`, forecast -2.5; -1.2 on PE (e10), forecast -1.3.

**The first FFN.** I took -1.2 for norm and FFN together; it is +1.2 in the changed kernel, +1.0 by e4's shift and +2.3 by its time, over my upper end of +0.7. The step "near DVE's own lead" was too kind: that ACT now runs the third SiLU behind the turned tiles, so that DVE and then the copy at 532.24 wait for it, was in the order's rows, and I costed it at nothing. Its price is the wait of 3.17 and 1.6 us of lower clock. That PE's two waits [rows 6] would go was right (the shift at 523 is 3.2 to 3.5 lower than at 460), and worth nothing, since 9 us later PE waited again for ACT and, behind it, DVE.

**RWKV.** Forecast -1.0, measured -2.8 (-1.0 to -5.3 by its interval). The sum had put the load at 1105.05 in another term; it alone brings 1.3 here. The other 1.0 that the traces show, between 960 and 980, has the size of my forecast by luck: I had it from the loads of the preparation, which bring nothing, and I had charged POOL's two moved splits with a loss of 0.4, while they are what brings it.

**The end of the mixer.** I took 0 between -2.4 and +1.3. In the changed kernel it is +0.9 up to the unit at 1155.89, near the replay's +1.3, and +1.8 by 1200, over my upper end. The mechanism of the replay, `w_lo` that block a low tile and a sum, is what the rows show (2.31 and 2.88), at more than the 1.2 to 1.5 that I gave each; my averaging it with a hope was wrong. That the affine steps and mixed tiles and the load share one wait of PE, so that their gains don't add, was nowhere in the sum.

By time the parts add: +5.6 (e1) + 2.3 (e4) - 2.8 (e12) + 1.1 (e3) = +6.2, against +7.2 measured; with intervals of 2.2 on each that agrees, and doesn't test more than the sum. Of the rivals, "nothing of it arrives" and the one of a longer table switch have no support: the exposed load is worth its 1.28. Of my signs, the first `o_scale`, the missing wait for `w_hi` and the long low tile came; the transposes came at 41.33 with three long steps, not near 39.1 with two.

## What to carry to other kernels

A chain of small dependent steps on VectorE beside long operations of GpSimd is priced by the number of such operations that fall into it, not by its own steps, and each one that it meets makes the next meeting likelier: replay it until the chain ends, then add what TensorE's clock costs if the wait gets long. A wait of TensorE is worth removing only up to the next point where it meets the same full engine; here the gains on TensorE at three places were gone within 35 us. Two gains that shorten the same wait don't add. Take a bundle apart before judging it: the whole cost 7.2 us, while its norm, table set, POOL's moved splits and mixed tiles, with its start repaired by two more moves (the sines and the chain), gained 4.8.

## What the runs showed of the hardware

Short operations on 16 partitions by 128 elements (0.21 to 0.28 us) were held 2.3 to 2.4 us by a GpSimd operation on other tiles, in the TENSOR_SCALAR form as well as in the TENSOR_TENSOR form (2.35 at 31.41 in e5). A wait of TensorE of 4.91 us was followed by the lower of its two clock levels, one of 3.17 by a shorter stretch of it (0.60 over 538 to 542), and one of 2.16 (at 1157.95 in the changed kernel) and one of 1.51 (e5) by none. The length of the one wait doesn't settle it, though: at the output norm of before the clock is at 0.50 from 469 on, behind waits of 0.57 and 1.05 and matmuls of one column. And in some executions the clock falls in the RWKV mixer between 1028 and 1035 (0.54 in e12, 0.77 in e7, 0.88 in e4) and in others it doesn't (1.00 in e9 and e10, which have e12's lists there); a single profiled execution can hide 1 to 2 us in that (e12 loses 2.1 from 1020 to 1035). A table load behind an ACTIVATE cost ACT its 1.28 and no more: the load begins at 1105.05, 0.01 behind the end of the ACTIVATE of 1104.35.
